# The opening of a two-layer diffusion step: the last two token tiles of x loaded later, the first norm made in two parts

## What is computed

```python
m = jax.nn.silu(cond) @ ada_w[layer] + ada_b[layer]        # 6 x 1024 modulation values, two conditions
h = rmsnorm(x, norm_g[layer, 0]) * (1 + sc1) + sh1
u_val, u_gate, q, k, v, g = jnp.split(h @ w_in, idx, axis=-1)
z = u_val * jax.nn.sigmoid(u_gate)                          # the gate columns are computed first
```

## Time and profile before

| | |
|---|---|
| median of 3 runs | 1571.56 us (1571.03 to 1571.68) |
| the profiled execution | 1571.34 us, its span 1569.5 us |
| mean granted TensorE clock | 0.996 of full |
| TensorE busy | 1546.9 us, 99% of the span |
| VectorE, ScalarE, GpSimd busy | 63%, 40%, 31% |

### The profile page before, as it was taken

The page is one execution under the profiler, slowest core; times in us unless marked ns, Lnnn a source line. Parts: engine busy times, 40 slices in busy tenths (PEclk is TensorE's granted clock), DMA queues, the critical chain, the costliest instruction groups (busy, mean ns, idle before and its releaser), DMA issues.

```text
span 1569.5 us, 28786 instructions
## 1 busy us (share of the span) xinstructions
PE 1546.9 (99%) x11992; PEld 1513.2 (96%) x11992; DVE 986.2 (63%) x1831; ACT 625.4 (40%) x1150; POOL 485.0 (31%) x350
## 2 busy tenths in 40 slices
PE   8999999999999999999999999999999999999998
PEld 7999999999999999999999999999999999999998
DVE  5338677675774755565555887773675755556555
ACT  5323333344432344234235534652443334523443
POOL 0223313314222344144235253101333344324431
PEclk9999999999999999999999999999999999999999
DMA  9454333313243344344344121001221232223212
GB/s 328 156 183 146 121 114 117 101 54 109 80 158 111 122 132 137 108 136 147 104 152 134 35 81 61 28 2 54 81 81 56 67 108 68 83 67 106 69 54 81
DMA packets 133410, 162.23 MB, mean 103 GB/s; under 512 B 4640, under 2 KB 108064, under 8 KB 133280
## 3 DMA queue, kind: packets, MB, share of 16 engines
q1 hardware_dynamic: 132048, 159.34, 31.6%
q10 hardware_dynamic: 1232, 1.05, 0.2%
HBM read 156.44 MB, written 3.93 MB: 102 GB/s over the span
## 4 chain that ended last, share of the span: by engine, by line
PE 89%; DVE 7%; ACT 2%; issue 1%; POOL 0%; DVEq 0%; ACTq 0%
PE ps L664 58%; PE ps L1083 19%; PE ps L783 3%; PE ps L1275 2%; PE ps L1223 1%; DVE ps L1895 1%; PE ps L920 1%; PE ps L953 1%; DVE hL L1906 1%; PE ps L869 1%; DVE ps L1885 1%; PE ps L949 1%; DVE amx L2492 1%; ACT wH L1319 1%; PE ps L1250 1%
## 5 line engine op out<-in xcount | busy, mean ns | idle before, releaser
L1820 POOL TENSOR_TENSOR wL<-raw,wH 128x512 fp32r<-128x512 f32 x212 | 312.0, 1496 | 713.2 <-ACT wH L1319 552.8
L664 PE MATMUL ps<-fH,wH 128*128 128x320 f32 x1024 | 318.4, 311 | 0.2 <-DVE fL L2278 0.2
L664 PE MATMUL ps<-fL,wH 128*128 128x320 f32 x1024 | 316.2, 309 | 0.0
L664 PE MATMUL ps<-fH,wL 128*128 128x320 f32 x1024 | 316.2, 309 | 0.0
L1856 DVE SCALAR_TENSOR_TENSOR xT<-ps,modT,xT 128x192 f32<-128x192 f32 (+1 forms) x456 | 183.4, 435 | 192.0 <-PE ps L664 190.2
L1820 POOL TENSOR_TENSOR wL<-raw_high,wH 128x512 fp32r<-128x512 f32 x124 | 164.0, 1348 | 338.6 <-ACT wH L1331 209.7
L664 PE MATMUL ps<-hH,wH 128*128 128x320 f32 x704 | 221.1, 314 | 2.0 <-DVE hL L1906 1.1
L664 PE MATMUL ps<-hH,wL 128*128 128x320 f32 x704 | 217.5, 309 | 0.0
L664 PE MATMUL ps<-hL,wH 128*128 128x320 f32 x704 | 217.5, 309 | 0.0
L664 PEld LDWEIGHTS ps<-fH,wH 128*128 128x128 f32 x1024 | 192.3, 188 | 3.4 <-DVE xT L1856 1.2
L664 PEld LDWEIGHTS ps<-fL,wH 128*128 128x128 f32 x1024 | 192.3, 188 | 0.1
(11 more groups left out here) (268 smaller groups left out, 3092.3 us busy)
## 6 DMA issues: line engine op xcount, KB each, us to landing
ada<-in_ada_w SPq DMA_DIRECT2D x40, 1024.0 KB, 5.2
raw<-in_mlp_w SPq DMA_DIRECT2D x64, 512.0 KB, 3.8
raw_high<-in_mlp_w SPq DMA_DIRECT2D x64, 512.0 KB, 3.8
raw<-in_even_w_in SPq DMA_DIRECT2D x28, 512.0 KB, 5.9
pre_w<-in_ada_w SPq DMA_DIRECT2D x16, 512.0 KB, 9.0
raw<-in_odd_w_qkv SPq DMA_DIRECT2D x10, 512.0 KB, 3.5
raw<-in_even_w_out SPq DMA_DIRECT2D x8, 512.0 KB, 3.5
raw<-in_odd_w_o SPq DMA_DIRECT2D x6, 512.0 KB, 3.5
```

Source lines behind the costliest of these rows:

```text
L664: last = nc.tensor.matmul(ps[:, bank, 0:width], a_, b_, start=(k == 0 and p_ == 0), stop=(k == nk - 1 and p_ == 2))
L1820: last = nc.gpsimd.tensor_tensor(wL[:, at % 4, cs], raw(t)[:, j, cs], wH[:, at % 4, cs].bitcast(F32), ALU.subtract)
```

## The change

SyncE issues the last two x tiles (3 and 4) behind modulation block 0 and the first halves of the two gate weight tiles, instead of directly behind tile 2. TensorE turns tiles 0 to 2 and makes their sums first, then the first strips and the 24 gate products of token half 0 with chunks 0 and 1; only then it turns tiles 3 and 4, makes their sums, and goes on with the second strips. The four transposition groups of tiles 3 and 4 go to PSUM banks 7, 5, 7, 5 (`X_BANK`), so the third and the fourth wait until VectorE has copied the first and the second. ScalarE squares tiles 3 and 4 behind the high part of the second weight half; VectorE copies them behind the low part of that weight half. No operation is added and none is dropped.

```diff
@@ TensorE's banks @@
+X_BANK = (0, 1, 2, 3, 0, 1, 7, 5, 7, 5)
@@ SyncE @@
-            for tile in range(NT):
+            for tile in range(3):
                 load_x(tile)
             gate_tiles = [k8(even_w_in[0], CONV + 256 * t) for t in range(2)]
             for j in range(2):
                 load_pre(j)
                 for t in range(2):
                     load_tile(T_GATE + t, gate_tiles[t], (j,))
+                if j == 0:
+                    load_x(3)
+                    load_x(4)
             load_pre(2)
@@ TensorE, x_turn @@
                 for q in range(2):
                     n = 2 * tile + q
-                    if n >= 4:
+                    if n in (4, 5):
                         pe.wait_ge(dve_free, n - 3)
+                    elif n > 7:
+                        pe.wait_ge(dve_free, n - 1)
+                    elif n == 7:
+                        pe.wait_ge(rstd_held, 1)
@@ TensorE, gate_step @@
                         if k == 0:
-                            if n < 4:
-                                pe.wait_ge(dve_free, G_GATE)
-                            elif n < 6:
+                            pe.wait_ge(dve_free, 6 if n < 4 else G_GATE)
+                            if n in (4, 5):
                                 pe.wait_ge(rstd_held, n - 3)
@@ TensorE, the order @@
-            for tile in range(NT):
+            for tile in range(3):
                 x_turn(tile)
-            for tile in range(NT):
+            for tile in range(3):
                 first_sums(tile)
             pe.wait_ge(siluc_ready, 1)
             pre_strip(0)
             gate_step((0, 1), (0, 1))
             gate_step((2, 3), (0, 1))
+            for tile in (3, 4):
+                x_turn(tile)
+            for tile in (3, 4):
+                first_sums(tile)
             pre_strip(1)
@@ ScalarE @@
-            for tile in range(NT):
+            def x_square(tile):
                 act.wait_ge(x_in[tile], 16)
...
-                if tile == 2:
-                    first_std(0, 3)
-            first_std(3, NT)
-            for half in range(2):
+            def rstd_copy(half):
                 act.wait_ge(rstd_full, half + 1)
                 nc.scalar.activation(rstd[:, half, :], ps[:, 5 + half, 0:HALF], ACT.Copy).then_inc(rstd_held, 1)
+            for tile in range(3):
+                x_square(tile)
+            first_std(0, 3)
+            rstd_copy(0)
             split(T_GATE, None, (0,))
             hi(0, 0, (0, 1))
             split(T_GATE + 1, None, (0,))
+            x_square(3)
+            x_square(4)
+            first_std(3, NT)
+            rstd_copy(1)
             hi(0, 1, (0, 1))
@@ VectorE @@
-            for n in range(8):
+            for n in range(6):
                 x_copy(n)
             first_rstd(0, 0, 3)
-            for n in range(8, 10):
-                x_copy(n)
-            first_rstd(1, 3, NT)
...
                     if j == 0 and half == 0:
                         weight_lo(T_GATE + 1, (0,))
+                        for n in range(6, 10):
+                            x_copy(n)
+                        first_rstd(1, 3, NT)
```

More of the change, by code:

```diff
@@ L814, in x_turn @@
                     n = 2 * tile + q
-                    if n >= 4:
+                    if n in (4, 5):
                         pe.wait_ge(dve_free, n - 3)
+                    elif n > 7:
+                        pe.wait_ge(dve_free, n - 1)
+                    elif n == 7:
+                        pe.wait_ge(rstd_held, 1)
                     for j in range(4):
                         c0 = (4 * q + j) * P
-                        last = nc.tensor.transpose(ps[:, n % 4, j * P:(j + 1) * P], x_nat[:, tile, c0:c0 + P], ident)
+                        last = nc.tensor.transpose(ps[:, X_BANK[n], j * P:(j + 1) * P], x_nat[:, tile, c0:c0 + P], ident)
                     last.then_inc(acc_full, 1)
@@ L1993, in x_copy @@
                 nc.vector.tensor_copy(xT[:, 4 * q:4 * q + 4, tile * P:(tile + 1) * P],
-                                      ps[:, n % 4, :].rearrange("p (k n) -> p k n", n=P)).then_inc(dve_free, 1)
+                                      ps[:, X_BANK[n], :].rearrange("p (k n) -> p k n", n=P)).then_inc(dve_free, 1)
             def first_rstd(part, t0, t1):
```

## The result

The changed kernel takes 1575.23 us in the median of 13 runs (1573.95 to 1576.07); the kernel before beside it 1571.40 us (1570.00 to 1572.09, 13 runs). The ratio is 1.0024, with a 95% interval of 1.0017 to 1.0031: slower by 3.8 us (0.24%). Forecast were 1574.7 us, within 1572.2 to 1576.7. The profiled execution took 1575.27 us with a span of 1573.5 us, 4.0 us more than the earlier trace rows.

A forecast was written before the change was run, and what follows sets the result against it. TensorE, busy 99% of the span, was taken as the bound, with a VectorE/ScalarE chain whose delayed start delays the kernel. Shift 2.85 + 0.3 = +3.15 us on 1571.34, plus 0.22 for the median: 1574.7 us, range 1572.2 to 1576.7.

The forecast's parts named there:

- Head start: Opening up to the first gate product: it starts at 20.7 (bounds 19.7 and 21.1) instead of 23.45, 2.75 us earlier.
- The 24 products: Gate products of token half 0 on TensorE: 5.2 us, between 3.76 at full clock and 6.7 at half.
- T0: End of the 24 products, when TensorE comes to the moved transpositions: forecast 25.9 (bounds 23.5 and 27.8).
- rival (4): All 24 products and the strips behind the hole at half clock: shift +4.1 to +5.2, 1575.7 to 1576.8; chance 0.14.
- The second part: Norm of tiles 3 and 4, now mid-kernel: h values of the second token half start at T0 + 4.75.
- What is late next: Behind those h values: 2.81 us, then a rigid 11.34 us VectorE/ScalarE chain, reaching T0 + 18.95, before 42.00.
- M: Start of the first product of feature chunk 4: 42.00 before, forecast at T0 + 18.95.
- Shift = T0 - 23.05: Delay of the whole kernel, computed from T0; +2.85 us with T0 at 25.9.
- The clock in the hole: TensorE between T0 and T0 + 4.2, mostly standing: clock may fall to half over the second strips, +0.3 us.
- (1): Head start is kept, the moved part hidden under the products: 1568.8 us if all 2.75 us stayed; chance 0.04.
- (2): Clock stays up over strips and products: shift +0.45 to about +2, 1572.0 to 1573.5 us; chance 0.12.
- (3): Block 0 quarters land as late as before: T0 28.64, shift 5.6, 1577.2 us; chance 0.04.

The follow-up runs named there:

- transfers alone: Kernel before with only SyncE's transfer order changed (x tiles 3 and 4 late), engines' order as before: 1579.74 us, ratio 1.0053.
- other banks: Changed kernel with the moved transposition groups in PSUM banks 7, 5, 4, 7, so the third needn't wait for a copy: 1574.99 us, ratio 1.0025.
- engines alone: Changed kernel with all five x tiles loaded first, so only the engines' order differs from the kernel before: 1577.86 us, ratio 1.0042.
- the warm one: Changed kernel with 13 products on ones between the first strips and the first gate product: 1572.21 us, ratio 1.0010.
- more copies: Kernel before with four more 128x512 VectorE copies, into an unread buffer, at the place to which the change moves its four: 1571.37 us, ratio 1.0001.
- the part moved earlier and the products warm: Changed kernel with banks 7, 5, 4, 7, moved transpositions 12 products earlier, and 13 products on ones ahead of the gate products: 1570.93 us, ratio 1.0000.

## Why the prediction was right

*Head start.* Right: first product at 20.58, forecast 20.7. The strips ended at 16.99 (17.2), since they ran partly at half clock, as assumed. The first weight half was there at 16.60 (16.7). x tile 4 landed only at 21.8 instead of 20.9, which cost nothing: ScalarE was done with it before 23.5, 3 us ahead of the transpositions. Why it took longer is open; with the transfers alone changed it was there at 20.81.

*The 24 products.* This term was mis-sized: 6.30 us instead of 5.2, T0 26.88 instead of 25.9. The clock was at half until about 26.2 (0.59 over the window from 23.40), 5.6 us behind the first product; before, it had risen 3.3 us behind it. The bound of 6.7 us at half clock was nearly reached. That is rival (4) in part: its T0 began at 27.1, its shift at 4.1. It is more than the whole difference between 3.15 and 3.88 us. The argument for 5.2, "since they start after a standing stretch as before", does not hold. Behind a stand of 3.6 us the same 24 products took 5.26 us (before), 5.66 (other banks), 6.28 (engines alone), 6.30 (changed) and 3.75 (transfers alone). No run shows what chooses among these, so a value near the middle was a fair guess, and no more.

*The second part.* T0 to the values of token half 1 took 4.94 us, forecast 4.75; the difference is VectorE's 0.21 us between the second and the third copy, which I had called covered. The run with other banks removes it (4.63 us).

*What is late next.* Right: T0 + 19.00 for M, forecast T0 + 18.95; this held in the runs with T0 at 23.58 and 29.91 too. "Shift = T0 - 23.05" gives 3.83 for the changed kernel (3.88 measured at M), 0.53 for the warm one (0.57) and 6.86 for the engines alone (6.90). The wait of TensorE ahead of M stayed 0.29 us and did not grow to 0.6; its products of token half 1 had begun late already (T0 + 7.3 instead of T0 + 7.0).

*The clock in the hole.* Wrong for the profiled execution: I added 0.3 us for half clock over the second strips, but they took 1.95 us at full clock. From 26.8 to 30.2 TensorE was busy for 2.12 of 3.4 us and stayed at 2.4 GHz, where 1.88 of 3.3 had been followed by half clock before. The Trainium skill ("TensorE: Matmul & The Clock Gate", What's actually happening) says that throttled is the default state and that activity releases the clock. The row from 20.00 agrees, which is at half clock from the end of the stand on that began at 16.99. The hole did not bring a fall. Nor did the stand from 18.64 to 22.22 in the kernel with more copies: the clock was at full in it and behind it. The error of +0.3 and that of -1.1 in the products partly cancel, and that is luck: without the +0.3 the forecast would have been 1 us low.

*The rivals.* (1) needed T0 below 23.05. The warm run came to 23.58 and stopped there; M came before 42.00 (at 41.16) only with the part moved earlier and the products warm. (2) is the warm run, 1572.2 us in the range given for it. (3) is what the run with the engines alone shows: without the head start, 1577.9 us against the 1577.2 computed.

## What to carry to other kernels

A load can be put off only as far as what hangs behind it can be: two tiles landed late, in time, but their way of transposition, copy, reciprocal, broadcast and copy again goes four times from engine to engine and takes 4.9 us here, from wherever TensorE's order puts it, with 14 us of chain behind. Before moving work "under" the products, look at where the issuing engine's own queue puts it: work issued behind the products is not under them. And count a head start by the clock as well; products that begin earlier, behind the same standing stretch, may run at half clock for longer (6.30 us against 5.26 here), and one profile does not tell what the next execution gets.

## What the runs showed of the hardware

TensorE's granted clock decided up to 2.5 us of this 4 us question. The 24 products of 128x320 took 3.76 us where 13 products on ones ran ahead of them. Without these they stood 3.6 us first, and took 5.26 us in the kernel before, 6.30 in the changed one and 3.75 in the run with the transfers alone. So the stand does not always bring half clock. In all three profiles with the 13 products the clock was full over the products behind them.

This is also seen in the runs without a profile. Of the 32 executions of the kernel before beside the last runs, 16 had a mean granted clock of 0.996 and a median of 1571.5 us, and 16 had 0.997 or 0.998 and a median of 1570.6 us.

By the medians the 13 products in a stand that exists anyway brought the changed kernel 2.5 us against the kernel before, and the kernel before 1.0 us, where the transfers of the next blocks took over as the bound (that interval takes in no change).

An x tile with rows of 4 KB took 1.32 us to pass (tiles 3 and 4 of the kernel before). The five transfers behind it, with rows of 1 KB, took 1.50 us each. All are 512 KB.
